# A fused two-block network on one core: memory values in token order, two tiles' convolution taps summed in SBUF, part of the mean on GpSimd, an earlier norm, and the next projection's first two tiles paired

## What is computed

```python
def causal_dwconv(x, w):            # 31 taps, one filter per channel
    ...
def conformer_conv(h, w_in, b_in, dw, dw_b, ln_g, ln_b, w_out, b_out):
    u = h @ w_in + b_in                               # 1024 -> 2048
    u = u[..., :D] * jax.nn.sigmoid(u[..., D:])
    u = causal_dwconv(u, dw) + dw_b
    u = jax.nn.silu(layernorm(u, ln_g, ln_b))
    return u @ w_out + b_out

def memory_cross_attention(h, memn, w_q, w_kv, w_o):  # memn: 256 memory tokens
    q = h @ w_q
    kv = memn @ w_kv                                  # keys | values
    s = (q . keys) / 16;  p = softmax(s);  o = p @ values
    return o @ w_o
```

## Time and profile before

| | us |
|---|---|
| median of 3 runs | 2369.77 |
| lowest, highest | 2369.59, 2373.05 |
| the profiled execution | 2371.05 |
| its span | 2369.3 |

### The profile page before, as it was taken

One profiled execution on the slowest core, in us unless ns is written; L12 is line 12 of the kernel. 1 busy time (PEld: TensorE's weight loads), 2 busy tenths in 40 slices (PEclk: granted clock), 3 DMA queues, 4 the chain that ended last, 5 costly groups with the idle time before them and its releaser, 6 DMA issues.

```text
span 2369.3 us, 35384 instructions
## 1 busy us (share of the span) xinstructions
PE 2311.9 (98%) x13666; PEld 1864.1 (79%) x13666; DVE 1108.4 (47%) x1870; ACT 982.3 (41%) x1671; POOL 1105.5 (47%) x952
## 2 busy tenths in 40 slices
PE   8999999999999999989999999999999999999998
PEld 6776678888867778869878888888787878888887
DVE  3446553113143887463334651652697333561562
ACT  5656652222256563444333231235665433322232
POOL 3433544444523342337525454445775625445344
PEclk9999999999999999999999999999999999999999
DMA  4211012222411210024212232222223212233222
GB/s 155 96 63 52 19 63 98 98 98 97 155 54 54 72 54 20 4 99 134 89 54 89 98 107 98 89 97 81 72 72 125 98 45 89 89 103 110 81 98 72
DMA packets 58479, 197.75 MB, mean 83 GB/s; under 512 B 6753, under 2 KB 11617, under 8 KB 57825
## 3 DMA queue, kind: packets, MB, share of 16 engines
q1 hardware_dynamic: 54000, 189.85, 23.8%
q10 hardware_dynamic: 4336, 5.96, 0.8%
HBM read 193.69 MB, written 2.10 MB: 83 GB/s over the span
## 4 chain that ended last, share of the span: by engine, by line
PE 52%; DVE 2%; POOL 1%; ACT 1%; issue 0%; DVEq 0%; POOLq 0%; ACTq 0%
PE ps L407 12%; PE ps L409 12%; PE ps L408 12%; PE ps L495 3%; PE ps L494 3%; PE ps L493 3%; PE ps L3225 1%; PE ps L3248 1%; DVE ps L3442 1%; POOL conv_y L3399 0%; PE ps L3455 0%; PE ps L3457 0%; PE ps L3456 0%; POOL w_lo L518 0%; PE ps L3235 0%
## 5 line engine op out<-in xcount | busy, mean ns | idle before, releaser
L517 POOL TENSOR_TENSOR w_lo<-raw,w_hi 128x512 fp32r<-128x512 f32 x342 | 448.4, 1311 | 899.9 <-ACT w_hi L509 899.9
L407 PE MATMUL ps<-ahead_hi,w_hi 128*128 128x512 f32 x1216 | 478.2, 393 | 0.3 <-DVE ahead_lo L784 0.3
L409 PE MATMUL ps<-ahead_hi,w_lo 128*128 128x512 f32 x1216 | 473.3, 389 | 0.0
L408 PE MATMUL ps<-ahead_lo,w_hi 128*128 128x512 f32 x1216 | 473.2, 389 | 0.0
L518 POOL TENSOR_TENSOR w_lo<-raw,w_hi 128x512 fp32r<-128x512 f32 x342 | 450.7, 1318 | 0.0
L509 ACT ACTIVATE w_hi<-raw 128x1024 fp32r<-128x1024 f32 x342 | 354.0, 1051 | 171.6 <-PE ps L495 90.3
L797 DVE TENSOR_TENSOR x_stream<-x_stream,ps 128x512 f32<-128x512 f32 x79 | 54.3, 688 | 459.7 <-PE ps L409 274.9
L407 PEld LDWEIGHTS ps<-ahead_hi,w_hi 128*128 128x128 f32 x1216 | 228.3, 188 | 50.2 <-issue 2.4
L408 PEld LDWEIGHTS ps<-ahead_lo,w_hi 128*128 128x128 f32 x1216 | 228.4, 188 | 49.3 <-issue 2.4
L409 PEld LDWEIGHTS ps<-ahead_hi,w_lo 128*128 128x128 f32 x1216 | 228.3, 188 | 47.6
L3590 ACT ACTIVATE ffn_s<-ps 128x512 f32<-128x512 f32 x44 | 26.4, 600 | 322.1 <-DVE ps L3618 322.1
(11 more groups left out here) (496 smaller groups left out, 4611.1 us busy)
## 6 DMA issues: line engine op xcount, KB each, us to landing
raw<-in_wall SPq DMA_DIRECT2D x346, 512.0 KB, 3.3
x_stream<-in_x SPq DMA_DIRECT2D x8, 256.0 KB, 5.3
out_y<-x_stream SPq DMA_DIRECT2D x16, 128.0 KB, 1.9
lora_a<-in_lora_a ACTq DMA_DIRECT2D x1, 1280.0 KB, 10.7
dist<-in_consts SPq DMA_DIRECT2D x1, 1088.0 KB, 8.0
lora_b<-in_lora_b ACTq DMA_DIRECT2D x1, 1024.0 KB, 5.2
mem<-in_mem SPq DMA_DIRECT2D x1, 1024.0 KB, 4.7
gwb<-in_lora_b SPq DMA_DIRECT2D x1, 1024.0 KB, 6.4
```

The lines of the kernel that those rows point to most:

```text
L407: pe.matmul(out, hi, src.hi[:, t, 0:width], start=first, stop=False)
L408: pe.matmul(out, hi, src.lo[:, t, 0:width], start=False, stop=False)
L409: return pe.matmul(out, lo, src.hi[:, t, 0:width], start=False, stop=last)
L517: e.tensor_tensor(self.w.lo[:, s, 0:512], self.raw[:, s, 0:512], as_float(self.w.hi[:, s, 0:512]), ALU.subtract)
```

## The change

- **Values in token order.** The value half of each memory projection takes the memory as the stationary operand and 512 weight columns as the moving one. The result has tokens on partitions, so transposes, their copies and `kv_turned` are gone. The weights of the value half are laid out anew (`by_tokens`). Two banks collect the columns of four chunks; ScalarE copies them out after the fourth.
- **Own taps.** The 19 VectorE taps of conv tiles 0 and 1 are summed in an SBUF tile `conv_own`: tile 0's first 16 steps alone, then both by turns, then tile 1's rest alone, each waiting for the step before it. Two more steps per tile add them to `conv_y` and then the bank. The steps don't wait for TensorE's taps.
- **Bounds.** `BOUNDS` counts 162 instructions and spreads them anew.
- **Mean.** GpSimd adds `conv_y` of tiles 0 to 3 in `ln_rt`, behind pairs 4, 6 and 7; TensorE does one mean matmul for them and four for the rest.
- **Order.** Mean, variance, square, root and Silu stand one to three chunks sooner in the second memory projection; Silu comes in two portions with a weight chunk between.
- **Paired.** The output projection after it makes its first two tiles together, input tile by input tile.

```diff
+    def two_tiles(self, pe, sums):
+        used, lo_r = self.marks[0], self.marks[3]
+        for q in range(self.kt):
+            pe.wait_ge(self.ready.sem, self.ready(q + 1))
+            for j in range(2):
+                if q == 0:
+                    pe.wait_ge(lo_r.sem, lo_r(j + 1))
+                mm = sums(self.k.ps[:, self.bank + j, 0:self.width], j, q, 0, q == 0, q == self.kt - 1)
...
+    def token_chunk(self, pe, m):
...
+        for q in range(2):
+            w, t = slice(q * 512, (q + 1) * 512), 2 * c + q
+            hi, lo = self.w.hi[:, s, w], self.w.lo[:, s, w]
+            for b in range(MEM // P):
+                out, at = k.ps[:, self.bank + 2 * half + b, :], slice(b * P, (b + 1) * P)
+                pe.matmul(out, src.hi[:, t, at], hi, start=(t == 0), stop=False)
+                pe.matmul(out, src.lo[:, t, at], hi, start=False, stop=False)
+                mm = pe.matmul(out, src.hi[:, t, at], lo, start=False, stop=(t == self.kt - 1))
+        mm.then_inc(used.sem, 1)
...
-    BOUNDS = (0, 0, 10, 28, 40, 58, 80, 98, 118)
+    DVE_TAPS = TAPS - PE_TAPS - POOL_TAPS
+    OWN_OPS, ALONE = 2 * (DVE_TAPS + 2), 16
+    BOUNDS = (0, 16, 32, 42, 60, 78, 98, 116, 134)
...
+    def own_step(self, v, m, step):
+        k, own, y = self.k, self.own[:, m, :], self.y[:, m, :]
+        t = PE_TAPS + POOL_TAPS + step
+        if step:
+            v.wait_ge(self.added.sem, self.added(self.own_added(m, step - 1)))
+        if step == 0:
+            v.tensor_scalar(own, self.u[:, m, t:t + T], self.tap(m, t), k.vec("cdw_b", m), ALU.mult, ALU.add
+                            ).then_inc(self.added.sem, 1)
+        elif step < self.DVE_TAPS:
+            v.scalar_tensor_tensor(own, self.u[:, m, t:t + T], self.tap(m, t), own, ALU.mult, ALU.add
+                                   ).then_inc(self.added.sem, 1)
+        elif step == self.DVE_TAPS:
+            v.wait_ge(self.pooled.sem, self.pooled((POOL_TAPS - 1) * (m + 1)))
+            v.tensor_tensor(y, y, own, ALU.add).then_inc(self.added.sem, 1)
+        else:
+            v.wait_ge(self.summed.sem, self.summed(m + 1))
+            v.tensor_tensor(y, y, k.ps[:, m, :], ALU.add).then_inc(self.kept.sem, 1)
...
+            if f in (4, 6, 7):
+                self.mean_pool(g, {4: 1, 6: 2, 7: 3}[f])
...
-        for m in {6: (0, 1, 2), 7: (3, 4, 5), 11: (6, 7)}.get(t, ()):
+        for m in {7: (3, 4, 5), 10: (6, 7)}.get(t, ()):
             self.mean_tensor(pe, m)
-        for m in {13: (0, 1, 2, 3), 14: (4, 5, 6, 7)}.get(t, ()):
+        for m in {11: (0, 1, 2), 12: (3, 4, 5, 6, 7)}.get(t, ()):
             self.variance_tensor(pe, m)
-        if t == 2 * KD - 1:
-            self.keys.turns(pe)
...
+        if m == 2 * KD - 1:
+            self.fed_scalar(act, 3, KD)
...
+        if m == 14:
+            self.fed_scalar(act, 0, 3)
```

More of the change, by code:

```diff
@@ L343, in __init__ @@
     def __init__(self, k, m_tiles, kt, src, act=None, vector=None, pool=None, width=T, feed=None, unroll=False,
-                 norm=False, bank=0, ready=None, prev=None, fill=None, release=False, middle=None, packed=False, held=0, early=0, norm_at=0, between=None):
+                 norm=False, bank=0, ready=None, prev=None, fill=None, release=False, middle=None, packed=False, held=0, early=0, norm_at=0, between=None, tokens=None, paired=False):
+        self.paired = paired
+        self.tokens = tokens
         self.held, self.early, self.norm_at, self.between = held, early, norm_at, between
@@ L444, in tensor @@
                 continue
-            for j in range(4):
+            if first_group and self.paired:
+                self.two_tiles(pe, sums)
+            for j in range(2 if first_group and self.paired else 0, 4):
                 if self.held and isinstance(i, int) and 4 * i + j == self.m_tiles - 1:
+                    continue
+                if self.tokens is not None and 4 * i + j >= self.tokens:
+                    self.token_chunk(pe, 4 * i + j)
+                    if self.fill is not None:
+                        self.fill(pe, 4 * i + j)
                     continue
@@ L3134, in taken @@
     def taken(self, act, bank, m):
-        act.wait_ge(self.used.sem, self.used(m + 1))
-        out = self.km[:, m, :] if m < KD else self.raw[:, m - KD, :]
-        act.activation(out, self.k.ps[:, bank + m % 4, 0:MEM], ACT.Copy).then_inc(self.free.sem, 1)
-    def turn(self, pe, t):
-        if t == 0:
-            self.turns(pe)
-        self.kept(pe, t)
-    def turns(self, pe):
-        k = self.k
-        pe.wait_ge(self.free.sem, self.free(2 * KD + RING))
-        for n in range(4):
-            mb, half = n % 2, n // 2
-            for q in range(4):
-                mm = pe.transpose(k.ps[:, 4 + n, q * P:(q + 1) * P], self.raw[:, 4 * half + q, mb * P:(mb + 1) * P], k.ident)
-            mm.then_inc(self.tr.sem, 1)
@@ L3167 @@
+    def kept(self, pe, t):
+        if t == 1:
+            pe.wait_ge(self.values.sem, self.values(MEM // P))
 class Attention:
@@ L3336, in __init__ @@
         self.tapped = diagonals.tile("conv_tapped", 2, T)
+        self.own = at(24).tile("conv_own", 2, T)
         self.tap_scaled, self.pooled = k.marks("taps_scaled", "pool_taps")
+        self.pooled_y = k.marks("conv_summed")
+        k.advance(3, "conv_summed")
         k.advance(KD * POOL_TAPS, "taps_scaled")
@@ new lines, in own_added @@
+    def own_added(self, m, step):
+        at, last = self.own_place(m, step), self.DVE_TAPS + 1
+        return at + 1 - sum(1 for n in range(2) if self.own_place(n, last) < at)
+    def own_step(self, v, m, step):
[12 more added lines that the diff above has]
+            v.tensor_tensor(y, y, own, ALU.add).then_inc(self.added.sem, 1)
+        else:
+            v.wait_ge(self.summed.sem, self.summed(m + 1))
+            v.tensor_tensor(y, y, k.ps[:, m, :], ALU.add).then_inc(self.kept.sem, 1)
@@ L3423, in taps_vector @@
     def taps_vector(self, v, first, last):
         k = self.k
-        for pair, n in (divmod(at, self.PAIR_OPS) for at in range(first, last)):
-            base = pair * (self.PAIR_OPS - 2)
+        for at in range(first, min(last, self.OWN_OPS)):
+            for m in range(2):
+                for step in range(self.DVE_TAPS + 2):
+                    if self.own_place(m, step) == at:
+                        self.own_step(v, m, step)
+        for pair, n in (divmod(at - self.OWN_OPS, self.PAIR_OPS) for at in range(max(first, self.OWN_OPS), last)):
+            pair += 1
+            base = 2 * self.DVE_TAPS * pair + 2
@@ L3707, in second_block @@
     assert room.at <= top + 24 * 1024
-    keys = MemoryKeys(k, km, vt, turned)
+    keys = MemoryKeys(k, km, vt)
     def keys_scalar(act, i, j):
```

103 lines of the change are left out of this document (70 added, 33 removed).

## The result

| | before | after |
|---|---|---|
| median | 2369.68 us (2368.45 to 2373.05, 4 runs) | 2388.99 us (2388.38 to 2389.91, 4 runs) |
| span of the profiled execution | 2369.3 | 2387.8 |
| mean granted TensorE clock | 0.991 | 0.986 |

The ratio is 1.0078, 95% interval 1.0066 to 1.009: 18.5 us slower. The forecast was 2388 us, from 2372 to 2396, and slower with a chance of 0.76.

The account below looks back on a forecast made before the run. TensorE was taken to bound the kernel. Values -3.4, SBUF port +14.5, bounds +7.2 and +5.3, second projection and its successor -5.1 gave +18.5 us: median 2388 us, range 2372 to 2396.

Follow-up runs that it names:

- e4: Changed kernel with own sums of tiles 0 and 1 in PSUM banks 2 and 3 and each pair opening one batch later; ratio to before 0.9979.
- e1: Changed kernel with the conv taps and BOUNDS of before put back, the other edits kept; median 2365.08 us, ratio to before 0.9979.
- e10: e4 plus w_hi split sooner, GpSimd's third mean add later, and taps of tiles 2 to 7 in rolling order; 2353.30 us, ratio to before 0.9934.
- e6: e1 with the output projection's first two tiles one after the other again instead of paired; ratio to before 0.9965.
- e5: e1 with all eight Silu pairs moved behind the w_hi split of the output projection's second chunk; ratio to before 0.9957.

## What to carry to other kernels

Moving sums from PSUM to SBUF to be free of a wait changes the operands' home as well as the order; where GpSimd reads SBUF beside it, the same order with the sums in a spare PSUM bank keeps the freedom and loses the price. What the freedom is worth is another question: here it was nothing (e4 against e1), and whether e10's rolling order needs it was not tried. An engine that works in order should begin nothing whose second step waits for an event later than what is queued behind it: batch 3's 17 instructions and batch 5's 15 together cost 13 us, for one semaphore each. When a step is made to need something sooner, as the paired tiles need the second chunk's weights, ask where in which engine's list it is made; here one split moved by three Silu pairs turned a loss of 1.1 to 2.2 us (e1 against e6) into a gain of 2.6 (e5 against e6).
